# Differential attention and rotary stage of a two-layer trunk: ScalarE takes DVE's copies, one softmax scaling and own buffers for the rounded y

## What is computed

```python
q_d, k_d, v_d = heads of h @ w_in           # 4 heads, two maps of 64 dims each
q_d, k_d = rope(q_d), rope(k_d)             # [x1*c - x2*s, x1*s + x2*c], latent tokens only
...
p = softmax(q1 @ k1.T) - lam * softmax(q2 @ k2.T)
o_d = rms(p @ v) * (1 - lam_init)
...
y = g_m * (o_m @ w_br_mlstm) + g_a * (o_a @ w_br_mla) + g_d * (o_d @ w_br_diff)
x = x + g1 * (y @ w_out)
```

## Time and profile before

| what | value |
|---|---|
| median of 3 runs | 2632.36 us (2631.67 to 2634.23) |
| the profiled execution's own time | 2634.0 us |
| its span, first to last instruction | 2632.2 us |
| PE busy | 2533.6 us, 96% |
| DVE, ACT, POOL busy | 1250.5, 750.8, 1330.7 us |
| mean granted clock of PE | 0.984 of 2.4 GHz |

### The profile page before, as it was taken

The page is one execution under the profiler, slowest core; times in us unless marked ns, Lnnn a source line. Parts: engine busy times, 40 slices in busy tenths (PEclk is TensorE's granted clock), DMA queues, the critical chain, the costliest instruction groups (busy, mean ns, idle before and its releaser), DMA issues.

```text
span 2632.2 us, 41789 instructions
## 1 busy us (share of the span) xinstructions
PE 2533.6 (96%) x17328; PEld 2367.1 (90%) x17328; DVE 1250.5 (48%) x1699; ACT 750.8 (29%) x1373; POOL 1330.7 (51%) x607
## 2 busy tenths in 40 slices
PE   5999999999999999999989999999999999999997
PEld 3989986888899999999978899778888999999997
DVE  5443255866735423132554523659565363132235
ACT  3251355213322303021222513550334123112031
POOL 2535530453356666666654466106434666666664
PEclk8999999999999999999998999999999999999999
DMA  6202224531121222222211122342111222222221
GB/s 262 71 22 68 73 103 161 189 117 41 41 73 65 73 76 77 72 74 80 73 64 49 36 68 74 127 165 71 64 41 49 72 73 73 72 81 73 73 75 63
DMA packets 62556, 215.34 MB, mean 82 GB/s; under 512 B 6688, under 2 KB 11168, under 8 KB 62112
## 3 DMA queue, kind: packets, MB, share of 16 engines
q1 hardware_dynamic: 56448, 203.97, 22.7%
q10 hardware_dynamic: 5920, 8.70, 0.9%
HBM read 208.15 MB, written 4.49 MB: 81 GB/s over the span
## 4 chain that ended last, share of the span: by engine, by line
PE 84%; DVE 7%; issue 3%; ACT 2%; POOL 1%; DVEq 1%; DMA 1%; SPq 1%; POOLq 0%; ACTq 0%
PE big L517 21%; PE big L520 21%; PE big L521 21%; PE four L703 3%; PE big L774 3%; PE four L786 2%; PE four L599 2%; PE four L805 2%; PE big L543 1%; PE big L726 1%; PE big L546 1%; PE big L547 1%; PE four L746 1%; DVE prob_d L1651 1%; DVE prob_d L1649 1%
## 5 line engine op out<-in xcount | busy, mean ns | idle before, releaser
L481 POOL TENSOR_TENSOR w_hi<-raw,cst 128x1024 fp32r<-128x1024 f32 x288 | 552.8, 1919 | 1177.5 <-PE big L517 886.6
L517 PE MATMUL big<-act_hi,w_hi 128*128 128x320 f32 x2528 | 790.3, 313 | 6.6 <-issue 5.6
L520 PE MATMUL big<-act_lo,w_hi 128*128 128x320 f32 x2528 | 785.3, 311 | 0.0
L521 PE MATMUL big<-act_hi,w_lo 128*128 128x320 f32 x2528 | 785.1, 311 | 0.0
L484 POOL TENSOR_TENSOR w_lo<-raw,w_hi 128x1024 fp32r<-128x1024 f32 x288 | 742.7, 2579 | 41.0
L517 PEld LDWEIGHTS big<-act_hi,w_hi 128*128 128x128 f32 x2528 | 478.6, 189 | 16.0 <-issue 14.7
L520 PEld LDWEIGHTS big<-act_lo,w_hi 128*128 128x128 f32 x2528 | 478.6, 189 | 0.7
L521 PEld LDWEIGHTS big<-act_hi,w_lo 128*128 128x128 f32 x2528 | 478.3, 189 | 0.0
L517 PE MATMUL big<-u_hi,w_hi 128*128 128x320 f32 (+1 forms) x1024 | 319.0, 312 | 1.9 <-DVE u_lo L2071 1.9
L520 PE MATMUL big<-u_lo,w_hi 128*128 128x320 f32 (+1 forms) x1024 | 317.4, 310 | 0.0
L521 PE MATMUL big<-u_hi,w_lo 128*128 128x320 f32 (+1 forms) x1024 | 317.1, 310 | 0.0
(11 more groups left out here) (306 smaller groups left out, 3832.8 us busy)
## 6 DMA issues: line engine op xcount, KB each, us to landing
raw<-in_w SPq DMA_DIRECT2D x368, 512.0 KB, 3.4
first_mod<-in_first SPq DMA_DIRECT2D x16, 512.0 KB, 15.7
x<-in_x ACTq DMA_DIRECT2D x1, 2560.0 KB, 13.1
out_y<-x SPq DMA_DIRECT2D x8, 320.0 KB, 2.6
cst<-in_const ACTq DMA_DIRECT2D x1, 1664.0 KB, 7.8
small<-in_small ACTq DMA_DIRECT2D x2, 437.0 KB, 9.2
out_C<-c_new ACTq DMA_DIRECT2D x2, 258.0 KB
v_d<-in_past ACTq DMA_DIRECT2D x2, 256.0 KB, 2.9
```

The lines of the kernel that those rows point to most:

```text
L481: nc.gpsimd.tensor_tensor(w_hi[:, to, :], raw[:, slot, :], ones[:, 0:1].to_broadcast([P, BLK]), ALU.mult)
L517: first = mm(ps, wh, ah, start=k == 0, stop=False)
L520: mm(ps, wh, al, start=False, stop=False)
L521: last = mm(ps, wl, ah, start=False, stop=k == nk - 1)
```

## The change

Four parts, in both layers.

1. Rotary stage: ACT makes the four crossed copies into `crossed[m % 2]` and the copy of the context tokens, between its copy of the tile and `raw_kept`; DVE keeps cos, one full-width sin and the add. ACT's row of modulation for tile 4 moves ahead of its wait for that tile.
2. Attention: the factor of the second map is multiplied with -lambda by DVE on one column; ACT applies it (`scale_second`); DVE's combination waits for `second_scaled`. ACT also copies the outputs. ACT's copy of the transposes goes between the exponentials of the two maps.
3. On PE only the fifth transpose waits for `out_copied` (LATE's wait moves to `values`).
4. y's parts: tiles 0 to 5 get buffers of their own, `y_hi` and `y_lo`; ACT rounds them between the gates, DVE makes each remainder one tile later.

```diff
+        crossed = [rs, sq[:,0,:]]
-        tanh_d = [stage[:, 0, :], stage[:, 1, :], prob_d[:, 2, :], prob_d[:, 3, :]]
+        tanh_d = [stage[:, 0, :], stage[:, 1, :], prob_d[:, 0, :], prob_d[:, 1, :]]
...
+        def y_tile(k):
+            return (y_hi[:, k, :], y_lo[:, k, :]) if k < 6 else (act_hi[:, k, :], act_lo[:, k, :])
...
                 def turn(i):
-                    if i:
-                        pe.wait_ge(out_copied, l * 20 + i)
                     for c in range(1 if t == LATE else 5):
+                        if c == 4 and i:
+                            pe.wait_ge(out_copied, l * 20 + i)
...
+                def scale_second(i):
+                    act.wait_ge(second_factor, l * 20 + i + 1)
+                    f(prob_d[:, c1, 0:w], prob_d[:, c1, 0:w], ACT.Copy, scale=row_sum[:, c1:c1 + 1]).then_inc(second_scaled, 1)
...
                 for i in range(-1, n):
+                    if i >= 1:
+                        outputs(i - 1)
                     if i + 1 < n:
-                        exps(i + 1)
+                        exps(i + 1, (0,))
                     if i >= 0:
                         half_gates(l, 2 * i + 2)
                         copyT(i)
+                    if i + 1 < n:
+                        exps(i + 1, (1,))
+                    if i + 1 < n:
+                        scale_second(i + 1)
                     half_gates(l, 2 * i + 3)
...
+                    for g in range(4):
+                        r, o = slice(32 * g, 32 * g + 32), slice(32 * (g ^ 1), 32 * (g ^ 1) + 32)
+                        f(crossed[m % 2][o, CTX:T], stage[r, m % 2, CTX:T], ACT.Copy)
+                    f(dst[:, 0:CTX], stage[:, m % 2, 0:CTX], ACT.Copy)
...
+                for gates, rounded in (((2, 3), range(0, 4)), ((4, 5), range(4, 6)), ((6, 7), range(6, 8))):
...
-                    v.tensor_scalar(p1, p1, row_sum[:, c0 + 1:c0 + 2], neg_lam, ALU.mult, ALU.mult)
+                    v.tensor_scalar(row_sum[:, c0 + 1:c0 + 2], row_sum[:, c0 + 1:c0 + 2], neg_lam, None, ALU.mult)\
+                        .then_inc(second_factor, 1)
+                    dve.wait_ge(second_scaled, l * 20 + i + 1)
...
-                    for g in range(4):
-                        v.tensor_tensor(t2[o, CTX:T], src[r, CTX:T], c_("sin_d", r), ALU.mult)
-                    v.tensor_copy(dst[:, 0:CTX], src[:, 0:CTX])
+                    v.tensor_tensor(t2[:, CTX:T], crossed[m % 2][:, CTX:T], c_("sin_d"), ALU.mult)
...
-                    for k in range(0, 6) if m == 5 else ([m] if m > 5 else []):
+                    for k in {0: (), 7: (6, 7)}.get(m, (m - 1,)):
```

More of the change, by code:

```diff
@@ L253, in trunk @@
         stage = sb("stage", [P, 2, T])
+        crossed = [rs, sq[:, 0, :]]
         A0 = base[0]
@@ L497, in block_start, with project @@
                 pe.wait_ge(split_ready, l * DENSE + b + 1)
-            def project(l, uses, first_block, tiles, nk, hi, lo, n=HALF, arrived=None, more=0):
+            def project(l, uses, first_block, tiles, nk, hi, lo, n=HALF, arrived=None, more=0, tile=None):
                 for p in range(tiles * nk):
@@ L1025, in _ @@
                 merge_d(l)
[L1028 to L1029 removed]
+                project(l, USE["wout"], FIRST_BLOCK["wout"], 8, KD, None, None,
+                        arrived=lambda k: l * SPLITS + FIRST_SPLIT["y"] + k + 1, tile=y_tile)
                 for c in range(FF_CHUNKS):
@@ L1095, in head_hi, with round_tiles @@
                 f(hi[:, h, :], tiles[:, h, :], ACT.Copy).then_inc(hi_done, 1)
-            def round_tiles(l, name, pairs, scale=None):
+            def round_tiles(l, name, pairs, scale=None, only=None):
                 for k, (hi, src) in enumerate(pairs):
+                    if only is not None and k not in only:
+                        continue
                     act.wait_ge(whole, l * WHOLES + FIRST_SPLIT[name] + k + 1)
@@ L1144, in exps @@
                         act.wait_ge(pT_ready, l * 60 + 40 + i - 1)
-                    for m in range(2):
+                    for m in maps:
                         ps, b, _ = buf(USE["da"][2 * i + m])
@@ L1175, in attend_d @@
                         head_square(l, (i - 6) // 5)
+                outputs(n - 1)
+                act.drain()
                 head_square(l, H_D - 1)
@@ L1492, in _ @@
                     use = USE["dq"][m]
+                    if l + 1 < DEPTH and m == 4:
+                        keep_row(l + 1, 0, one[0][:, 0:256])
                     wait_ready(act, l, use)
@@ L1520, in _ @@
                     head_hi(l, "od", q_d, od_hi, h)
-                for m in range(2, 8):
-                    gate_of_d(l, m)
-                round_tiles(l, "y", [(act_hi[:, k, :], y[:, k, :]) for k in range(KD)], scale=0.5)
+                y_pairs = [(y_tile(k)[0], y[:, k, :]) for k in range(KD)]
+                for gates, rounded in (((2, 3), range(0, 4)), ((4, 5), range(4, 6)), ((6, 7), range(6, 8))):
+                    for m in gates:
+                        gate_of_d(l, m)
+                    round_tiles(l, "y", y_pairs, scale=0.5, only=rounded)
                 f(u_hi[:, :, T:T + 2], mods[:, l, 24:32, :], ACT.Copy).then_inc(shift_hi, 1)
```

38 lines of the change are left out of this document (22 added, 16 removed).

## The result

The changed kernel takes 2597.85 us (median of 4, 2596.29 to 2600.6), the kernel before 2632.3 on the same chip: ratio 0.9869, 95% interval 0.9852 to 0.9886.

The account below looks back on a forecast made before the run. PE was taken as the bound, so only its waits and half-clock time could fall: 7.8 (rotary stage) + 7.0 (wout) + 3.6 (attention) = 18.4 us, giving 2614.0 us, own range 2606 to 2622, 80% within 2602 to 2625.

Parts of the forecast that it names:

- Rotary stage, 7.8: Crossed copies to ACT: 6.4 us at the start of dv in layer 1, 1.4 at layer 0's row copy.
- wout, 7.0: Start of wout: per layer 3.0 us wait and 1.5 half clock gone, 1.0 new stall at tile 6; range 5 to 9.
- Attention, 3.6: Differential attention: only the longest stall before the transposes goes, 1.8 us a layer; bounds gain 16, loss 8.
- I take those two as even: Attention: slack exceeded by 1.3 us when DVE operations are held, set against the earlier copy and transposes freed from DVE's output.
- slack of 2.3: Attention, undisturbed unit: DVE's combination ends 8.1 us after the next unit's scores and is wanted at 10.4.
- the four-column product: Attention: DVE operation on four columns, 2.39 us in both its records, from which the narrow product's possible hold was priced.
- The offloading that I weighed: Attention scaling moved from DVE to ACT: by rule 0.14 us lost each, 5.6 in all; nothing kept in the sum.
- Copy one exponential sooner: Attention: ACT's copy of the transposes comes 1 us earlier, removing several waits for it; counted within the even balance.
- C: Rival: attention loses nearly all stalls through the copy's place and late wait, 15 us instead of 3.6, 2603; 18%.
- A: Rival: attention's DVE-ACT handover becomes the wait, narrow product and combination both held by POOL; slower, 2640; 10%.
- B: Rival: wout's wait only moves, remainders 6 and 7 both held, 2.8 us at tile 6 a layer; 2619; 12%.
- D: Rival: no gain in the rotary stage, ACT being the bound at over 7.05 us a tile; 2620; 3%.

Follow-up runs that it names:

- e9: Changed kernel plus one small DVE product a unit, four columns of a constant into an unread buffer, ahead of the one-column product: 2609.89 us.
- e17: Changed kernel with the scaling on DVE, factor made on one column first, the wide product writing its accumulator to an unread column: 2602.91 us.
- e5: Changed kernel with the second map scaled by DVE again, outputs and copy order as changed: 2608.55 us.
- e3: Changed kernel with ACT's copy of the transposes behind both exponentials again: 2605.86 us.
- e8: Kernel before with one edit, ACT's copy of the transposes between the two exponentials: 2630.61 us, ratio 0.9987.
- e4: Changed kernel with PE waiting for out_copied ahead of all five transposes again: 2597.44 us.
- e7: Changed kernel with scaling and output copy both on DVE again, leaving only the copy's place and the late wait of the attention's part: 2610.44 us.
- e13: Changed kernel plus three small constant DVE products a unit, outputs unused (one column, five columns, four columns apart): 2618.47 us, run once.
- e14: Changed kernel with the scaling on DVE, its 640 columns walked even ones first, then odd ones: 2608.41 us.

## Why the prediction was wrong in size

- *Rotary stage, 7.8*: 7.8 measured, in both places that I named. Crossed copies 0.64 us (I took 0.6), the small one 0.31 (0.4), dv 1.15 us behind dk (1.1), no half clock.
- *wout, 7.0*: 8.1. The term that was off is the new wait at tile 6, 0.58 us instead of 1.0 in layer 0. DVE's add and remainder were held, but for less than two whole steps.
- *Attention, 3.6*: 16.2. The step that failed is "the narrow product in the scaling's place can be held as long. Then the slack is exceeded by 1.3", and with it "I take those two as even". With one column the product is never held (40 of 40), so of the two holds in a row, 3.6 us together, one is left. It is at most 1.51 us over the 0.885 undisturbed, inside the slack of 2.3 that I had worked out. So the very arithmetic that I wrote down gives no waits for the combination, and the transposes indeed have none. The slack itself was counted well: in the clear unit with its scores at 613.07 the combination ends at 620.88, 7.8 us behind them, where I had 8.1. e9 comes near the world that I priced: attention 11.8 us worse, which would have left about 4.4, near my 3.6. I had also expected that the transposes would wait for the combination alone and that the stage would last 150 to 154 us. They wait for nobody, what is left at the values is a wait for ACT's copy, and the work of the 154.1 us of layer 0 takes 145.7.
- *The nearest row was the wrong one.* The earlier trace rows also held the reciprocal of two columns, 165 to 168 ns in 40 records, never held. I took the four-column product because it was the same operation and the dearer bound. The Trainium skill (VectorE: DVE Perf Modes, What auto-detection actually checks) gives this operation the mode with two ports by the outermost dimension that is longer than one element. One column has no such dimension; that it stays out of the mode is my reading of the page, which does not name the case. And the Trainium skill (SBUF — State Buffer, Who interferes with whom) excepts the form that writes its accumulator. The runs agree with both: 0.214 us for one column, 1.93 at most for four, 0.88 flat in e17.
- *The offloading that I weighed*: on ACT the scaling takes 0.83 us, more than the 0.75 assumed and the 0.61 on DVE, yet e5 shows 9.5 us for it. What decided was 2.25 under POOL, not the median. The rule by which I had each of 40 scalings lose 0.14 us went by the clear durations; for those it holds (0.61 against 0.83), for the time it does not. I had both figures and kept nothing for it in the sum.
- *Copy one exponential sooner*: worth 5.5 in the changed kernel (e3), 0.5 alone (e8) by the attention, 8.0 and 3.0 by the medians. The late wait: 0.0 beside ACT's outputs (e4), 1.6 to 3.3 with DVE's (e7 against e8, without and with the half-clock stretch).
- *Rivals*: C came true in size, 16.2 us for its 15, with 18%; its reason was half right, since it named the copy and the late wait and not the scaling. A's mechanism, with four columns, is e9; it costs 12 us there and still leaves the attention 4.4 us shorter than before, where A had it 23 longer. B and D did not occur.
- *Clock at the layers' starts*: 2.4 of the 34.5 us, in code that the change does not touch. I had no term for it; whether it is chance or an effect of earlier times is open. Among the nineteen profiled executions, before and changed kernel included, the stretch in layer 0 is within 0.1 us of the changed kernel's in six and 2.4 to 2.8 us longer in thirteen. The six all have the new rotary stage and the new y, and so have eight of the thirteen; the attention's part is present and absent in both groups. That code runs before any that the change edits, so an effect of the change on it isn't shown, nor excluded.

Together: 18.4 + 12.6 (attention, 1.7 of it the half-clock stretch of layer 0) + 1.1 (wout) + 2.4 (clock at the starts) = 34.5.

What is left in the attention is 3.6 us of stalls a layer, five of them; three, of 0.86, 0.67 and 0.39 us, were there before in nearly the same length. The longest, in PE's timeline, then DVE's and ACT's:

```profile
681.13 1.05 PE L759 MATMUL four<-probT_d,v_d 128*128 128x128 f32 x7 [1.07 <-ACT probT_d L1179]
...
676.49 1.82 DVE L1664 TENSOR_TENSOR y<-y,t 128x320 f32<-128x320 f32 x1
678.40 1.55 DVE L1681 TENSOR_REDUCE cols<-big 128x1 f32<-128x640 f32 x2
...
679.32 0.80 ACT L1169 ACTIVATE prob_d<-big,cols 128x640 f32<-128x640 f32 x1 [4.38 <-DVE cols L1681]
680.38 0.70 ACT L1179 ACTIVATE probT_d<-four 128x640 f32<-128x640 f32 x1 [0.17 <-issue]
```

POOL holds DVE's add, 1.82 instead of 0.49, so the maximum is late, ACT idles 4.38 us, and the copy stands behind that exponential although the transposes ended at 678.0.

## What to carry to other kernels

Price an operation by a row of its own form, width included: here four columns for one turned a term by 12 us. Where two engines exclude each other, judge a move by the longest duration in the chain and count how many operations in a row can be held; a slower form or engine that is never held (0.88 or 0.83 us against 0.61 with 2.25 at most) was the better one. Parts of a change are not worth the same alone and together: by the attention the copy's place gave 0.5 us alone and 5.5 with DVE freed (3.0 and 8.0 by the medians).

## What the runs showed of the hardware

- DVE's `TENSOR_SCALAR` from SBUF to SBUF is held by a POOL step from two SBUF inputs when it has four, five or 640 columns, strided or not (up to 1.93 us in e9, 2.15 in e13, 2.25 in e5 and e14, and 2.33 for the four apart in e13), never with one (0.213 to 0.216 us in 40). Narrow ones that began in the last 0.14 us of a step took no longer. `RECIPROCAL` of two columns takes 0.165 to 0.168 us, in 40 records before and 40 in the changed kernel, and is never held.
- The same product with its accumulator written out takes 0.88 us instead of 0.61 for 640 columns and is never held (e17).
- ACT's scaling took no longer under POOL: 0.827 to 0.832 us, inside a step or clear.
